# Moving 24 modulation blocks of a two-block transformer kernel from a merge stage into a feed-forward stage

## The reference

```python
def first_block(x, c, ctx, c_ctx, w_mod, b_mod, ...):
    for l in range(2):
        ...                                    # norm, modulation, four branches
        merged = sum(sigmoid(g) * (br @ w_branch[i]) ...)   # "merge": 4 branches, 8 tiles each
        x = x + gate * (merged @ w_out)
    return rmsnorm(x, final_norm_w)

def second_block(x, c, ada_w, ada_b, norm_g, ffn_w_up, ...):
    c_act = silu(c)
    for i in range(2):
        mod = c_act @ ada_w[i] + ada_b[i]                  # 6 * 1024 numbers
        sh_m, sc_m, gt_m, sh_f, sc_f, gt_f = split(mod, 6)
        h = rmsnorm(x, norm_g[i, 0]) * (1 + sc_m) + sh_m
        y = rglru_mixer(h, ...) if i == 0 else gla_mixer(h, ...)
        x = x + gt_m * rmsnorm(y, norm_g[i, 1])
        h = rmsnorm(x, norm_g[i, 2]) * (1 + sc_f) + sh_f
        u = causal_dwconv(h @ ffn_w_up[i], conv_w, conv_b)  # width 3, 2 * 2816 channels
        g, val = split(u, 2)
        x = x + gt_f * rmsnorm((gelu(g) * val) @ ffn_w_down[i], norm_g[i, 3])
```

## Time and profile before

| | |
|---|---|
| median of 3 runs | 1734.52 us (1733.71 to 1735.17) |
| the profiled execution | 1734.11 us, span 1732.3 us, mean granted clock 0.996 |
| TensorE busy | 1689.6 us, 98% of the span |
| VectorE busy | 1392.7 us, 80% |
| ScalarE busy | 883.6 us, 51% |
| modulation blocks on DVE, L2226 (96 of ada_w) | 119.8 us, mean 1280 ns |
| weight splits on DVE, L2190 | 489.8 us, 432, mean 1141 ns |
| mean DMA rate | 174 GB/s |

### The profile page before, as it was taken

How to read it: one execution, slowest core, us unless ns; L and a number is a source line. 1 busy time by engine, 2 the same in 40 slices (tenths; PEclk the granted TensorE clock), 3 DMA queues, 4 the chain that set the end, 5 groups by cost and what they waited for, 6 DMA issues and landing times.

```text
span 1732.3 us, 28134 instructions
## 1 busy us (share of the span) xinstructions
PE 1689.6 (98%) x10612; PEld 1475.4 (85%) x10612; DVE 1392.7 (80%) x2532; ACT 883.6 (51%) x1530; POOL 0.2 (0%) x4
## 2 busy tenths in 40 slices
PE   7999999999999999999999999999999999999998
PEld 4788887777888888898888999999899888889997
DVE  7799996546789998889787689877898767779874
ACT  5322324456333233453346755568766657566663
POOL 0000000000000000000000000000000000000000
PEclk9999999999999999999999999999999999999999
DMA  9683211211667776645333289744555544346553
GB/s 342 216 310 100 92 55 49 97 38 37 234 235 258 246 264 229 232 149 168 102 119 98 82 280 321 267 134 153 191 198 195 183 158 153 117 146 209 195 192 111
DMA packets 224774, 301.32 MB, mean 174 GB/s; under 512 B 6000, under 2 KB 188656, under 8 KB 224256
## 3 DMA queue, kind: packets, MB, share of 16 engines
q1 hardware_dynamic: 224640, 299.52, 51.6%
HBM read 298.45 MB, written 1.05 MB: 173 GB/s over the span
## 4 chain that ended last, share of the span: by engine, by line
PE 88%; DVE 6%; ACT 3%; issue 2%; DMA 1%; DVEq 0%; ACTq 0%
PE bank L706 21%; PE bank L711 21%; PE bank L708 21%; PE bank L1092 4%; PE bank L1094 3%; PE bank L1093 3%; PE bank L682 2%; PE bank L683 2%; PE bank L684 2%; DVE w_lo L2190 2%; PE bank L937 1%; PE bank L948 1%; PE bank L960 1%; PE bank L1159 1%; PE bank L1222 1%
## 5 line engine op out<-in xcount | busy, mean ns | idle before, releaser
L2190 DVE TENSOR_TENSOR w_lo<-ring,w_hi 128x1024 fp32r<-128x1024 f32 (+1 forms) x432 | 489.8, 1141 | 174.7 <-ACT w_hi L1408 172.5
L1408 ACT ACTIVATE w_hi<-ring 128x1024 fp32r<-128x1024 f32 (+1 forms) x432 | 425.6, 991 | 182.9 <-PE bank L711 90.4
L706 PE MATMUL bank<-h_hi,w_hi 128*128 128x256 f32 (+2 forms) x2086 | 372.9, 321 | 1.4 <-ACT w_hi L1408 1.4
L711 PE MATMUL bank<-h_hi,w_lo 128*128 128x256 f32 (+2 forms) x2086 | 366.9, 318 | 0.3
L708 PE MATMUL bank<-h_lo,w_hi 128*128 128x256 f32 (+2 forms) x2086 | 366.6, 318 | 0.0
L706 PEld LDWEIGHTS bank<-h_hi,w_hi 128*128 128x128 f32 x2086 | 305.1, 188 | 34.9 <-issue 2.7
L711 PEld LDWEIGHTS bank<-h_hi,w_lo 128*128 128x128 f32 x2086 | 305.8, 188 | 30.4 <-DVE w_lo L2190 0.7
L708 PEld LDWEIGHTS bank<-h_lo,w_hi 128*128 128x128 f32 x2086 | 305.8, 188 | 29.8
L1395 ACT ACTIVATE work<-bank 128x512 f32<-128x512 f32 (+1 forms) x134 | 67.2, 520 | 244.2 <-PE bank L711 164.2
L1395 ACT ACTIVATE arena<-bank 128x256 f32<-128x256 f32 (+4 forms) x119 | 55.2, 468 | 199.1 <-PE bank L711 122.0
L2492 DVE SCALAR_TENSOR_TENSOR arena<-arena,params 128x512 f32<-128x512 f32 (+1 forms) x240 | 130.5, 614 | 0.0
(11 more groups left out here) (320 smaller groups left out, 2116.5 us busy)
## 6 DMA issues: line engine op xcount, KB each, us to landing
ring<-in_w_in SPq DMA_DIRECT2D x86, 1024.0 KB, 5.5
arena<-in_ada_w_t SPq DMA_DIRECT2D x96, 512.0 KB, 5.9
ring<-in_ffn_w_up SPq DMA_DIRECT2D x44, 1024.0 KB, 5.0
ring<-in_ffn_w_down SPq DMA_DIRECT2D x20, 1024.0 KB, 5.1
ring<-in_w_branch SPq DMA_DIRECT2D x32, 512.0 KB, 4.7
arena<-in_w_mod_t SPq DMA_DIRECT2D x32, 512.0 KB, 4.9
ring<-in_gla_w_in SPq DMA_DIRECT2D x12, 1024.0 KB, 5.2
ring<-in_w_out SPq DMA_DIRECT2D x8, 1024.0 KB, 6.4
```

The costliest lines, as they stand in the source:

```text
L706: pe.matmul(out[:, 0:n], w[0][:, k, :], hi(k, n), start=k == 0, stop=False)
L711: m = pe.matmul(out[:, 0:n], w[1][:, k, :], hi(k, n), start=False, stop=k == tiles - 1)
L1408: nc.scalar.activation(hi, src, ACT.Copy)\
L2190: step(nc.vector.tensor_tensor(lo, src, hi.bitcast(F32), ALU.subtract), f"lo {u}", *(["used " + stream[w_units[u][0]][0]] if w_units[u][3] ...
```

## The change

Blocks 24 to 47 of layer 1's `ada_w` leave the merges. Twelve of them go into the up projection of ffn 0, one at the end of each i = 0 to 9 and two at the end of i = 10. Twelve go into its down projection, two after each of the splits of units 49, 51, 53 (first half of the columns) and 59, 61, 63 (second half). SP issues their DMAs right behind the slabs "w ffv 0.i" and behind the slabs "down 0.0.0", "0.0.2", "0.0.9", "0.1.2", "0.1.4" and "0.1.9". The first four blocks wait for `lo n3 0.7`; each later one waits for the block four before it. The slots of these 24 lie at another place of the arena, some buffers move by 48 columns, the row for the gains of three of the four norms gets a place of its own, and `modulation2(1)`, which turns the blocks into gains, is split into two calls, the second at the end of ffn 0.

```diff
+LATE_ADAS, UP_STAGE, DOWN_STAGE = 24, "up", "down"
+DOWN_AT = {"down 0.0.0": 0, "down 0.0.2": 1, "down 0.0.9": 2, "down 0.1.2": 3, "down 0.1.4": 4, "down 0.1.9": 5}
+DOWN_ADAS = ("0.5", "0.7", "0.9", "1.4", "1.6", "1.8")
...
-        for pair in range(1, pairs):
-            mod_plan[1, pair] = take_blocks(adas, 2 if pair >= KT // 2 else 0)
+        for i in range(11):
+            mod_plan[UP_STAGE, i] = take_blocks(adas, 2 if i == 10 else 1)
+        for i in range(6):
+            mod_plan[DOWN_STAGE, i] = take_blocks(adas, 2)
...
 # SP, right after the DMA of slab `name`:
+                if name.startswith("w ffv 0") or name[2:] in DOWN_AT:
+                    at = (UP_STAGE, int(name.split(".")[1])) if name.startswith("w ffv 0") else (DOWN_STAGE, DOWN_AT[name[2:]])
+                    for m in mod_plan[at]:
+                        i = mod_slot_of[m] - MOD_SLOTS
+                        mod_block(m, "%s %d.%d" % mod_order[i] if i >= len(mod_order) - LATE_ADAS else f"lo n3 0.{KT - 1}")
...
 # DVE, ffn(l), at the end of each i:
                         if 0 <= n < KT or n >= 2 * KT:
                             low_part(f"ff {l}.{n}", ff_part(1, n), ff_act[:, n, :], ff_part(0, n))
+                    if l == 0:
+                        mod_blocks(mod_plan[UP_STAGE, i])
...
 # DVE, down projection:
+                def late_adas(c):
+                    for i, at in enumerate(DOWN_ADAS if l == 0 else ()):
+                        if at[0] == c:
+                            split_to(unit_of[f"down 0.{at}"])
+                            mod_blocks(mod_plan[DOWN_STAGE, i])
+                late_adas("0")
                 split_to(unit_of[f"down {l}.1.2"])
                 for t in range(ST):
                     row_stored(tag, 0, t)
                     row_totalled(tag, t)
+                late_adas("1")
                 split_to(unit_of[f"down {l}.1.10"])
+                if l == 0:
+                    modulation2(1, (1,))
```

More of the change, by code:

```diff
@@ L295, in program @@
         yT = carve(0, KT, S)
-        xb_pad = carve(4096, KT, S + RG_K - 1)
-        xc, gel, rr, tt_, ix, a2 = (carve(6168 + 2048 * i, KT, S) for i in range(6))
+        xb_pad = carve(4096 + BESIDE, KT, S + RG_K - 1)
+        xc, gel, rr, tt_, ix, a2 = (carve(6168 + BESIDE + 2048 * i, KT, S) for i in range(6))
         lv = carve(0, 8, GLA_H * S)
@@ L307, in program @@
         head_sums, head_dev, head_inv = (carve(17664 + 8 * i, 8) for i in range(3))
-        ff_act = carve(4096, FT, S)
+        ff_act = carve(4096 + BESIDE, FT, S)
         ff_hi, ff_lo = (arena_r[:, c:c + (FT - 2 * KT) * S].rearrange("p (t s) -> p t s", s=S)
-                        for c in (9728, 9728 + (FT - 2 * KT) * S))
+                        for c in (9792, 9792 + (FT - 2 * KT) * S))
         def ff_part(lo, n):
@@ L384, in y_rows, with row_diag @@
             return yT[:, 4 * t:4 * t + 4, :]
-        row_diag, fin_row = c2_row, carve(2048 + BESIDE, D)
+        fin_row = carve(2048 + BESIDE, D)
+        early_diag = carve(2048 + BESIDE + D, D)
+        def row_diag(tag):
+            return c2_row if tag == "ffn 1" else early_diag
         z_hi, z_lo = (arena_r[:, c:c + P].rearrange("p (t s) -> p t s", t=KT) for c in (2048, 2048 + P))
@@ L508, in mod_slot @@
         def mod_slot(m):
-            return carve(12576 + D * (mod_slot_of[m] % MOD_SLOTS), D)
+            at = 13312 if mod_slot_of[m] >= len(mod_order) - LATE_ADAS else 12576
+            return carve(at + D * (mod_slot_of[m] % MOD_SLOTS), D)
         def mod_in(m):
@@ L1039, in gain_rows @@
                     for j in range(4):
-                        m = pe.matmul(out[:, P * j:P * j + P], ones_pp, row_diag[:, 512 * i + P * j:512 * i + P * j + P],
+                        m = pe.matmul(out[:, P * j:P * j + P], ones_pp, row_diag(tag)[:, 512 * i + P * j:512 * i + P * j + P],
                                       start=True, stop=True)
@@ L1851, in gain_diag @@
                 l, q = gain_of[tag]
-                nc.scalar.activation(row_diag[:, P * n:P * n + P], ident, ACT.Identity,
+                nc.scalar.activation(row_diag(tag)[:, P * n:P * n + P], ident, ACT.Identity,
                                      scale=gain2[l][:, q, n:n + 1])\
@@ L1961, in _ @@
                 if n == 0:
-                    act.wait_ge(*vector.did("gain2 1"))
+                    act.wait_ge(*vector.did("gain2 1.0"))
                 gain_diag("rg", n)
@@ L2074, in _ @@
             for n in range(GLA_H * ST):
+                if n == 0:
+                    act.wait_ge(*vector.did("gain2 1.1"))
                 gain_diag("ffn 1", n)
@@ L2253, in modulation1, with modulation2 @@
                 after(f"gain1 {l}.{a}")
-            def modulation2(l):
-                after(f"ada {l}.47")
+            def modulation2(l, parts=(0, 1)):
                 g = param("norm_g", 2, 4)
-                for q in range(2):
+                for q in parts:
                     c = 24 * q
+                    after(f"ada {l}.{c + 23}")
                     step(nc.vector.scalar_tensor_tensor(gain2[l][:, 2 * q, :], mod2[l][:, c + 8:c + 16], 1.0,
@@ L2263, in modulation2 @@
                     step(nc.vector.tensor_tensor(gain2[l][:, 2 * q + 1, :], mod2[l][:, c + 16:c + 24],
-                                                 g[:, l, 2 * q + 1, :], ALU.mult), *([f"gain2 {l}"] if q else []))
+                                                 g[:, l, 2 * q + 1, :], ALU.mult), f"gain2 {l}.{q}")
             def decays():
@@ L2755, in _ @@
                     modulation2(0)
-                    after("gain2 0")
+                    after("gain2 0.1")
                     step(nc.vector.tensor_tensor(fin_w2, param("fin_w"), param("fin_w"), ALU.mult))
@@ L2954, in _ @@
             step(nc.vector.memset(xb_pad[:, :, 0:RG_K - 1], 0.0), "xb z")
-            modulation2(1)
+            modulation2(1, (0,))
             dve.wait_ge(*scalar.did("dev n2 0"))
```

## The result

| | median of the runs | range | ratio to before, 95% interval |
|---|---|---|---|
| before (4 runs) | 1734.12 us | 1730.57 to 1735.17 | |
| changed (4 runs) | 1744.39 us | 1741.33 to 1747.98 | 1.0065 [1.0053, 1.0077] |

The forecast was 1739.5 us, slower, range 1731 to 1745. The direction holds, the size does not: the loss is 10 us where 5 were expected (the interval of the ratio is 9 to 13 us). The profiled execution took 1741.33 us (span 1739.6, mean granted clock 0.993), 7.2 us more than the profiled execution before (1734.11).

What follows compares the result with a forecast made beforehand. It took TensorE as the bound, held back by VectorE only at the merges' end: 1734.1 - 6.0 + 2.0 + 0.2 + 6.5 + 2.3 = 1739.1, put at 1739.5 us against the runs' median, range 1731 to 1745.

Steps and rivals of the forecast that it cites:

- Leaving the merges, -6.0: End of layer 1's merges: without the blocks TensorE's wait and the slow clock behind it go, 6.0 us gained.
- Start of ffn 0, +2.0: SP's wait for `lo n3 0.7` delays slab "w ffg 0.1", so TensorE stalls 2.0 us ahead of unit 4.
- the third rival: Clock falls at both gaps and VectorE enters late, with 3 us at ffn 0's start: 1745 us, chance 0.12.
- the 2.82 us one: TensorE's wait in the kernel before, at the end of layer 1's merges until 1110.91, with the clock falling after it.
- Up projection, +0.2: Up projection of ffn 0: VectorE, with a block per i, barely keeps up with TensorE; price 0.2 us (0 to 0.8).
- Turn, +6.5: Turn to the down projection: slab "down 0.0.4" queues behind both blocks of i = 10, making unit 48 late, 6.5 us.
- the chain with VectorE's best reserve: Turn, VectorE's reserve at 4.2 us: slab 0.0.4 issued 1362.9, landed +6.5, unit 48 ready 1371.6, 5.6 us late.
- Behind unit 48, +2.3: Down projection: either unit 54 is 1.9 us late at full clock or the clock falls, costing 3 us; price 2.3.

Runs made afterwards that it cites:

- experiment 5: The changed kernel measured once more, unedited, on another chip job: median 1748.60 us, 1.0063 of the kernel before.
- experiment 1: Changed kernel, four blocks issued behind slabs down 0.0.4 and 0.0.6 instead of 0.0.0 and 0.0.2: 1740.46 us, 1.0032 of the kernel before.
- experiment 3: Changed kernel with both order edits, at the down projection's slabs and at the start of ffn 0: 1733.87 us, 0.9988 of the kernel before.
- experiments 1 to 3: Changed kernel with down order edited (1740.46 us), with blocks 0 and 1 both behind slab w ffv 0.1 (1740.48 us), and with both edits (1733.87 us).
- experiment 6: Changed kernel, both order edits, one block instead of two at i = 10, later blocks regrouped in the down projection: 1731.48 us, 0.9970 of before.
- experiment 4: Changed kernel whose 24 moved blocks sum only 128 of 1024 columns, DMAs, waits and order kept: 1742.83 us, 1.0042 of the kernel before.
- 7: Changed kernel with filler matmuls, 5 ahead of unit 4 and 13 ahead of unit 48: 1748.32 us, 1.0064 of the kernel before.
- 9: Changed kernel with 5 filler matmuls ahead of unit 4 only: 1745.87 us, 1.0061 of the kernel before.
- experiment 10: Three more profiles of the kernel before, nothing changed: 1732.24, 1739.66 and 1732.04 us.

## Why the prediction was wrong in size, step by step

The mechanism was forecast; the sizes of three terms failed. The gain was priced from one execution, the low clock at the start of ffn 0 was put at nothing, and the landing of slab 0.0.4 was taken too short.

- **Leaving the merges, -6.0.** Right for the execution it was read from: 6.4. Over four executions the place cost 4.1 in the mean, so the mechanism was sound and the price from a single execution was not; this is some 2 us of the error in the median.
- **Start of ffn 0, +2.0.** The wait and its chain (SP behind `lo n3 0.7`, slab, ScalarE, unit 4) came as written, 2.3 us, with a landing of 7.0 us for the 6.7 taken; in experiment 5 it was 2.7 us idle. What failed is the clause against the third rival, that no wait here is as long as the 2.82 us one and that the clock so holds. The clock fell for 3.4 us behind 2.13 us of idle time: +1.7, which the sum left out. The step is 4.0 us. By the fit of the Trainium skill ("DMA: Bandwidth & Descriptors", Anatomy of one DMA), an estimate, block and slab would have taken 5.6 us and the stall 0.4; from the block's issue at 1233.89 to the slab's landing were 7.4. The page gives that fit for single DMAs issued by GpSimd, and these are two issued by SyncE, with a third right behind, so the difference says only that the fit does not carry over to them. The same section's statement that the issuing sequencer waits, not the DMA engines, agrees with the trace: no slab slipped past a block that waited.
- **Up projection, +0.2.** 0: TensorE has no gap in the 109 us behind 1243, with VectorE busy 107.59 (98.74 before). The 12 matmuls fewer in that window (952 for 964) are the half clock.
- **Turn, +6.5.** Right in place and mechanism, 7.1 in size. TensorE is 2.2 us earlier here than in the old trace (its unit 43 too), so the slab's issue at 1360.67 is 1362.9 in times of the old trace, exactly as the chain with VectorE's best reserve had it. That chain gave 5.6 us; slab 0.0.4 then took 7.9 us to land and not 6.5, which makes 7.0. Slab 0.0.6 was issued 0.5 us behind it; whether that slowed it was not tested.
- **Behind unit 48, +2.3.** One or the other, as written: the clock fell (2.1 us), and no wait at unit 54. In experiment 1, where the clock held, the wait at unit 54 was 1.6 us for the 1.9 estimated; in experiment 3 it was 1.5.
- **Together.** Losses 13.2 us for 11.0, gain 6.4 for 6.0: +6.8 in the profiled execution, where 5.0 were forecast and 7.2 came. The median's +10 has the smaller mean gain in it: 13.2 - 4.1 = 9.1. Of the 5 us by which the forecast was short, some 2 are the gain, 1.7 the clock at the start, 0.3 and 0.6 the two waits; the last us is within the scatter described below, and how it divides was not settled.

That SP's order, not VectorE's load or the traffic alone, makes most of the loss is shown by experiments 1 to 3: 10.7 of 13.4 us; the other 2.7 are VectorE late behind its blocks, and experiment 6 takes them out by giving it room. That VectorE's load sizes the wait at the turn is shown by 4. That nothing is gained by holding the clock up while the waits stay is what 7 and 9 show; that the clock at the start costs nothing in the end, because the turn gives it back, is argued from their traces.

## What to carry to other kernels

A wait put into a DMA issuer's program holds back all that is queued behind it, also where its own transfer is not urgent: look for the first transfer behind it whose buffer is due soon, and move the waiting one behind that; here two edits of order were worth 10.7 us in the traces of ffn 0 and 13 by the medians. When a step moves to another stage, ask for its instances at the first and the last tiles and at the turn of stages; those in the middle of the up projection and in the second half of the down projection were free. Before a difference of a few us is priced from one profiled execution, read the same spot in two or three more.

## What the runs showed that was not expected

**Two paces of TensorE at a granted clock of 1.00.** For a whole stage, matmuls that move 256 columns, each with its own weights, start either about 113 or about 118 ns apart. The window from 1255 to 1340 us in the kernel before and in the second profile of experiment 10:

```profile
1255.00:1340.00 85.00, 85.00 (x752) 85.00 (x752) 76.16 (x150) 56.84 (x96) 0.00 (x0) 1.00 0.60 197
```

```profile
1255.00:1340.00 85.00, 85.00 (x724) 85.00 (x723) 73.07 (x147) 53.96 (x92) 0.00 (x0) 1.00 0.61 197
```

TensorE is busy throughout and the clock full, but 724 matmuls pass instead of 752. Experiment 1 has 724 there too. The timeline of the second of these shows groups of eight 0.94 to 0.95 us apart, where the kernel before has 0.91:

```profile
1301.27 1.11 PE L706 MATMUL bank<-h_hi,w_hi 128*128 128x256 f32 x8
1302.22 1.10 PE L708 MATMUL bank<-h_lo,w_hi 128*128 128x256 f32 x8
```

Over the up projection's 1056 matmuls this is 4.6 us, and the stretch of ffn 0 is 192.66 us for 188.01. It occurs in kernels with and without the change, in the merges, ffn 0 or ffn 1, and stays for whole stages as a rule (two profiles of experiment 10 have both paces in the merges, 645 and 651 matmuls in 75 us where the others have 664 or 639); matmuls of 512 columns kept 227 ns in every profile. Of the 7.6 us between the second and third profiles of experiment 10 it makes 4.6 in ffn 0 and most of another 2.3 in the merges. That it also makes the spread of the runs without a profile is likely and not shown: of 30 of the kernel before 22 lay between 1732.62 and 1735.99 us and eight between 1737.20 and 1739.84. A single time says little here. What draws the pace stays open.

**The same idle time does not always lower the clock.** Just ahead of the merges, near 998 us, TensorE idles 1.9 us in every execution read; behind it the clock fell to 0.50 for 3.4 us in 4 of 14: the changed kernel's first profile, those of experiments 3 and 9 and the second of experiment 10. At the merges' end it fell behind 1.98 us and not behind 1.44, for 3.4 us behind 2.79 and for 6.8 behind 2.82. In experiment 4 it did not fall behind the 2.8 us at the turn. So the length of one idle time did not decide it, and the forecast's comparison with the 2.82 us could not.
